# Order of one expert block: gate and up, turn of the next rows, turn of the product, down at once

## What is computed

```python
def expert_block(args):
    xb, e = args                       # xb: 128 x 1024 rows of tokens
    hb = jax.nn.silu(xb @ w_gate[e]) * (xb @ w_up[e])      # 128 x 256
    return hb @ w_down[e]              # 128 x 1024

y = lax.map(expert_block, (x_pad, blk_expert)).reshape(P, D) * c_pad[:, None]
out = jax.ops.segment_sum(y, tok_pad, num_segments=T + 1)[:T]
```

## Time and profile before

| | us |
|---|---|
| median of 3 runs | 3321.82 |
| lowest and highest | 3316.71, 3329.70 |
| profiled execution, its own time | 3328.78 |
| span of the profiled execution | 3326.9 |
| TensorE matmul busy in the span | 2884.3 (87%) |
| VectorE busy | 1799.1 (54%) |
| ScalarE busy | 1037.0 (31%) |
| mean granted TensorE clock | 0.932 of 2.4 GHz |

### The profile page before, as it was taken

How to read it: one execution, slowest core, us unless ns; L and a number is a source line. 1 busy time by engine, 2 the same in 40 slices (tenths; PEclk the granted TensorE clock), 3 DMA queues, 4 the chain that set the end, 5 groups by cost and what they waited for, 6 DMA issues and landing times. The chain is left out here.

```text
span 3326.9 us, 35125 instructions
## 1 busy us (share of the span) xinstructions
PE 2884.3 (87%) x13216; PEld 2188.8 (66%) x13216; DVE 1799.1 (54%) x2548; ACT 1037.0 (31%) x1329; POOL 201.8 (6%) x142
## 2 busy tenths in 40 slices
PE   4999999999999987583998979898999989488883
PEld 4878777778877856462776955656575667366662
DVE  4687787778433214522434257666665763455554
ACT  3233333333222122431444122222121331355541
POOL 0010011111000000010111010000000000300002
PEclk8999999999999998796999989999989999699997
DMA  3111111111232101168110200000001032889986
GB/s 100 45 39 51 45 45 31 46 45 39 83 146 67 46 21 33 57 208 266 44 44 19 75 13 21 14 21 5 30 1 64 1 73 107 298 338 352 343 338 234
DMA packets 165549, 319.79 MB, mean 96 GB/s; under 512 B 12373, under 2 KB 120022, under 8 KB 152200
## 3 DMA queue, kind: packets, MB, share of 16 engines
q1 hardware_dynamic: 154408, 279.79, 24.8%
q10 hardware_dynamic: 5616, 20.45, 1.5%
q0 software_dynamic: 5360, 17.33, 1.4%
HBM read 271.91 MB, written 79.18 MB: 106 GB/s over the span
## 5 line engine op out<-in xcount | busy, mean ns | idle before, releaser
L445 PE MATMUL PS<-UHI,WHI 128*128 128x512 f32 x1008 | 415.2, 412 | 30.3 <-DVE arena L767 15.5
L445 PE MATMUL PS<-ULO,WHI 128*128 128x512 f32 x1008 | 402.2, 399 | 0.0
L445 PE MATMUL PS<-UHI,WLO 128*128 128x512 f32 x1008 | 402.1, 399 | 0.0
L445 PEld LDWEIGHTS PS<-UHI,WHI 128*128 128x128 f32 x1008 | 191.7, 190 | 82.1 <-issue 39.4
L1375 PE MATMUL PS<-U2HI,WHI 128*128 128x512 f32 x384 | 157.8, 411 | 75.0 <-POOL WLO L126 75.0
L445 PEld LDWEIGHTS PS<-ULO,WHI 128*128 128x128 f32 x1008 | 191.9, 190 | 46.8 <-issue 4.1
L445 PEld LDWEIGHTS PS<-UHI,WLO 128*128 128x128 f32 x1008 | 191.5, 190 | 46.8
L1929 ACT ACTIVATE arena<-PS,small 128x128 f32<-128x128 f32 (+7 forms) x128 | 94.8, 741 | 240.1 <-DVE small L2002 240.1
L1827 PE MATMUL PS<-arena 96*128 96x512 f32 (+3 forms) x384 | 162.5, 536 | 3.7 <-DVE arena L1989 2.9
L781 DVE SCALAR_TENSOR_TENSOR RC<-arena,cols,RC 128x1024 f32<-128x1024 f32 x120 | 157.4, 1311 | 9.9 <-issue 0.5
L781 DVE SCALAR_TENSOR_TENSOR arena<-arena,cols 128x1024 f32<-128x1024 f32 x120 | 156.6, 1305 | 9.5
(11 more groups left out here) (427 smaller groups left out, 5726.6 us busy)
## 6 DMA issues: line engine op xcount, KB each, us to landing
arena<-in_w_in SPq DMA_DIRECT2D x88, 512.0 KB, 3.9
y_dram<-arena ACTq DMA_DIRECT2D x33, 512.0 KB, 9.3
arena<-in_w_gate SPq DMA_DIRECT2D x13, 1024.0 KB, 5.6
arena<-in_w_up SPq DMA_DIRECT2D x13, 1024.0 KB, 9.0
arena<-in_w_down SPq DMA_DIRECT2D x13, 1024.0 KB, 11.0
RB<-xd_dram SPq DMA_DIRECT2D x22, 512.0 KB, 12.6
arena<-in_w_out SPq DMA_DIRECT2D x32, 256.0 KB, 2.7
RB<-in_w_gate SPq DMA_DIRECT2D x7, 1024.0 KB, 6.7
```

Of the source, the lines that this page charges most:

```text
L445: last = pe.matmul(o[:, h * HALF:(h + 1) * HALF], x[:, k, :], y[:, k, h * HALF:(h + 1) * HALF], start=(k == r == 0), stop=(k == ND - 1 and ...
```

## The change

TensorE's order becomes gate_up(b), turn(b+1), turn_hidden(b), down(b). ScalarE's becomes upper(b+1), silu(b), rows_hi(b+1), store(b), with one wait for the blocks' table (`s_blk`) ahead of upper(1). VectorE's becomes lower(b+1), gated(b), hidden(b), rows_lo(b+1). SP's and GpSimd's lists stay as they are.

```diff
 TensorE
                 turn(0)
                 for b in range(NS):
+                    gate_up(b)
                     if b + 1 < NS:
                         turn(b + 1)
-                    gate_up(b)
-                    if b:
-                        down(b - 1)
                     turn_hidden(b)
-                down(NS - 1)
+                    down(b)
 ScalarE
                 rows_hi(0)
                 for b in range(NS):
                     if b + 1 < NS:
-                        rows_hi(b + 1)
+                        if b == 0:
+                            act.wait_ge(s_blk, 1)
                         upper(b + 1)
                     silu(b)
-                    if b:
-                        store(b - 1)
-                store(NS - 1)
+                    if b + 1 < NS:
+                        rows_hi(b + 1)
+                    store(b)
 VectorE
                 rows_lo(0)
                 for b in range(NS):
                     if b + 1 < NS:
-                        rows_lo(b + 1)
                         lower(b + 1)
                     gated(b)
                     hidden(b)
+                    if b + 1 < NS:
+                        rows_lo(b + 1)
```

## The result

The changed kernel takes 3374.6 us in the median of 4 runs (3366.4 to 3382.9) against 3325.8 us of the kernel before, measured beside it (4 runs). The ratio is 1.0149, with a 95% interval of 1.0109 to 1.0189. The forecast was 3346, with a range up to 3368: the sign was right, the size half of what was measured.

The account below looks back on a forecast made before the run. Rows asked for only when the down of two blocks earlier ended were taken to bound the kernel. End +12.9, start -6.7 and clock losses +17.6 gave +23.8 us on the 3321.8 median: 3346, range 3322 to 3368.

Parts of the forecast that it names:

- (a): Expert stage: asking for rows to turning them now spans three blocks, some 20 us, 6.8 a block; waits for rows vanish.
- (b): Expert stage: new loop from down through store, upper, lower, gated and hidden turn to next down, 12.25 us a block.
- (c): Start of expert stage: gate_up(0) no longer stands behind turn(1), so down(0) comes 6.7 us earlier.
- (d): End of expert stage: down(0) to down(32) takes 391.0 us against 378.1, 12.9 more; the last interval is 11.25.
- (e): TensorE between gate_up and down: a 3.1 us lull drops the clock in one block of three, 11 x 1.6 = 17.6 us.
- 0 and one in two: Bounds on the share of blocks whose lull before down loses TensorE's clock; one in three was taken.
- the losing group: Old kernel's TensorE lulls of 3.4 us or more between down and gate_up: six of 11 lost the clock.
- The first: Expert stage: the 12.25 us loop holds but the clock stays up; +6.2 us, 3328; chance 0.22.
- The second: Expert stage: the new loop does not close, TensorE's own 11.25 us a block sets the pace; 3297; chance 0.10.
- The third: Expert stage: every lull loses the clock, 31 x 1.6 = 49.6 us; +55.8, 3378; chance 0.07.
- The fourth: Expert stage: rows still land last and the pace stays 11.8 us a block; 3322; chance 0.06.
- 10.9 us a block: Expert stage: least time for one block's 4.19 million bytes of transfers at the DMA engines' 384 GB/s.

Follow-up runs that it names:

- the swap on SP: Kernel before, with SP asking for rows(b-1) ahead of weights(b) instead of behind them: 3260.6 us, 0.9816; the same in the changed kernel: 3367.2 us, 1.0142.
- version with two copies on the short circle: Changed kernel with each product's store issued by SP, not ScalarE, plus two unused VectorE copies between lower and gated: 3332.0 us, 1.0027.
- the version with the filler: Changed kernel plus one unused 384-column matmul per block between turn(b+1) and the hidden turn: 3330.1 us, 1.0027.
- the cut circle: Changed kernel with ScalarE's store of the last block moved behind the rounding of the next weights (upper): 3296.3 us, 0.9922.

## Why the prediction was right in sign and too small

**(a) The rows' circle opens: right.** No turn waits for rows in the changed kernel, and the swap on SP, which takes 60 us off the kernel before, does nothing to it.

**(b) The new circle: right in every link, 0.14 us short.** Forecast 12.25, measured 12.39: `down` to store 3.71 (forecast 3.64), to upper 1.50 (1.49), to lower 1.09 (1.08), to gated 4.55 (4.54), to the hidden turn 0.47 (0.48), to the copy 0.54, to `down` 0.53 (0.48). The two links that were short are those in which a `down` starts after a wait; the prediction saw 0.07 of that and put it into the range, not into the value. Gated starts where lower ends (2999.62), not where silu ends (2998.48), as it said. The missing 0.14 us are worth 31 x 0.14 = 4.3 us.

**(c) Start: right.** From the first turn to `down(0)` are 14.3 us, 21.5 before: 7.2 us sooner, forecast 6.7.

**(d) End: right.** The last interval is 11.24 us, forecast 11.25.

**(e) The clock: the term that was mis-sized.** The prediction took 11 falls of 1.6 us, 17.6 us. There were 22 of 1.70 us (5.37 against 3.67), 37.4 us. That is 19.8 of the 23.6 us by which the sum was short; the circle's 4.3 are most of the rest. The price was near, and they fell into `down` as it said. The count was wrong, and the step that failed is the bound "0 and one in two". It counted falls among the unequal waits of the old kernel (six of eleven long ones) and took that share as the most there is; in the changed kernel 22 of 31 lulls of one length lost it. It also treated the lulls as so many chances; in the trace the losing blocks follow each other in a regular round, two or three and then one that kept the clock. What sets that round stays open. The version with two copies on the short circle has the circle and the lull that the forecast had (12.22 and 3.11 us): it lost the clock 5 times in its trace, not 11. So at its own lull the forecast looks too high, and at the real one, 0.15 us longer, it was far too low. The prediction said that "an error of 0.3 us in the circle would put them in the losing group"; half of that error was enough.

Put together: -7.2 for the start, 31 x 12.39 + 11.24 = 395.3 against 378.1 before, +17.2, and 22 x 1.70 = +37.4: +47.4 us, and 447.1 - 399.7 = 47.4 were measured in the profiled executions (medians: +48.9). The forecast's sum had +23.8.

**The rivals.** The first, circle without falls, is the version with the filler: 1.0027, forecast 3328 and measured 3330. The second, TensorE's own path, is what the cut circle gives: forecast 3297 and 11.25 us a block, measured 3296 and 11.26. Both were priced rightly and not what happened; the first with some luck, since its circle was 4.3 us too short as well. The third, a fall in every block, came nearer to the time (3378) than the forecast did, though 9 of the 31 kept the clock. The fourth fell with (a).

The Trainium skill's page "TensorE: Matmul & The Clock Gate", section "HAM oscillation — how this bites in real kernels", describes a loop in which the wait between two groups of matmuls throws the clock back in every single round. This trace agrees for 22 of 31 rounds and not for the other nine. The waits of the page's loop are also longer, 3 to 5 us each for a transfer; here the two waits of a lull are 1.15 and 0.56 us, with transposes around them.

One bound of the prediction was wrong without harm: 10.9 us a block as the limit by the transfers. The swapped kernel runs at 9.94. The weights of the first five blocks wait for no `down`, so the 32 intervals carry only the other 28 loads of weights, and the DMA engines moved 394 GB/s and not 384. By these figures the 28 loads, the rows, the stores and the residual are some 125 MB, about 318 us for the 32 intervals (an estimate), and 318.2 were measured.

## What to carry to other kernels

When an order by hand moves a consumer forward ("down at once"), write out the new circle link by link across all engines, and look at which instruction stands behind the one that waits: here the store's copy ahead of the next rounding closed a circle of 12.4 us through three engines, and moving that one store back took 78 us off. Then look at how TensorE's waits are spread: one lull of about 3 us at the same place in every block cost the clock in 22 of 31 blocks here, and the price of 1.7 us is paid where the circle is tightest. Here 0.6 us less in the circle, or useless work in the lull, took all of it away. And before reordering compute to hide a late transfer, look at what that transfer queues behind.

## What the runs showed that was not expected

- The number of clock falls does not grow smoothly with the lull: none of 31 at 2.7 and 2.9 us, 5 at 3.1, 22 at 3.27, 19 at 3.5 us. At 3.27 us the falls come in a regular round, two or three blocks that lose the clock and one that keeps it.
- Useless work made a kernel faster: one 384-column matmul in each block took 44 us off (37 between the traces), and eight transposes did the same within the measurement (1.0027 and 1.0043, intervals that overlap).
- 0.2 us more in every block's circle changed the time by nothing (1.0149 and 1.0150), because falls of the clock went away with it.
- Swapping two issues on SP, with not one byte or instruction more or less, gave 1.8%.
